# A second issuer for the expert weights: the second matrix from GpSimd's queue, the first from SyncE's

## The reference

```python
def moe_ffn(x2, w_router, b_router, w_mlp1, b_mlp1, w_mlp2, b_mlp2):
    logits = x2.astype(F32) @ w_router.astype(F32) + b_router.astype(F32)
    top_val, top_idx = lax.top_k(logits, TOP_K)        # 4 of 32
    gate = jax.nn.softmax(top_val, axis=-1)
    ...
    def expert_block(args):
        tok, gb, e = args
        hmid = x2[tok] @ w_mlp1[e] + b_mlp1[e]         # 1024 x 2048
        glu = jnp.minimum(hmid[:, :D_FF], SWIGLU_LIMIT)
        lin = jnp.clip(hmid[:, D_FF:], -SWIGLU_LIMIT, SWIGLU_LIMIT)
        act = glu * jax.nn.sigmoid(SWIGLU_ALPHA * glu) * (lin + 1.0)
        y = act @ w_mlp2[e] + b_mlp2[e]                # 1024 x 1024
        return y.astype(F32) * gb[:, None]
```

## Time and profile before

| | us |
|---|---|
| median of 3 runs | 1462.99 (1461.76 to 1463.04) |
| the profiled execution | 1465.3 |
| its span | 1463.5 |
| PE busy | 1387.0 (95%) |
| DVE busy | 444.8 (30%) |
| ACT busy | 271.6 (19%) |
| POOL busy | 24.5 (2%) |
| queue q1, share of 16 DMA engines | 79.1%, 458.29 MB |
| queue q0, share of 16 DMA engines | 1.4%, 5.40 MB |

### The profile page before, as it was taken

How to read it: one execution, slowest core, us unless ns; L and a number is a source line. 1 busy time by engine, 2 the same in 40 slices (tenths; PEclk the granted TensorE clock), 3 DMA queues, 4 the chain that set the end, 5 groups by cost and what they waited for, 6 DMA issues and landing times.

```text
span 1463.5 us, 18983 instructions
## 1 busy us (share of the span) xinstructions
PE 1387.0 (95%) x6775; PEld 775.3 (53%) x6775; DVE 444.8 (30%) x1164; ACT 271.6 (19%) x534; POOL 24.5 (2%) x54
## 2 busy tenths in 40 slices
PE   8999998998999999999999999999999999999998
PEld 6887777896477534434434344344343443434433
DVE  3035333534751222221321222213212132122222
ACT  4222732211302101111111011111110101101111
POOL 3000000000000000000000000000000000000000
PEclk9999988999999699999999999999999999999999
DMA  8753222113396299999999999999999999999996
GB/s 269 232 173 123 85 88 69 49 58 122 115 323 225 95 407 400 419 416 418 418 418 417 417 419 418 419 416 416 419 418 419 416 418 418 418 418 416 419 417 253
DMA packets 119362, 464.38 MB, mean 317 GB/s; under 512 B 7555, under 2 KB 43501, under 8 KB 86512
## 3 DMA queue, kind: packets, MB, share of 16 engines
q1 hardware_dynamic: 117632, 458.29, 79.1%
q0 software_dynamic: 1520, 5.40, 1.4%
q10 hardware_dynamic: 176, 0.22, 0.1%
HBM read 459.09 MB, written 5.83 MB: 318 GB/s over the span
## 4 chain that ended last, share of the span: by engine, by line
PE 73%; DMA 13%; SPq 6%; DVE 4%; ACT 2%; issue 2%; DVEq 0%; ACTq 0%
PE bank L612 69%; DMA ring<-in_w_mlp 12%; SPq L483 6%; PE bank L616 4%; DVE arena L2013 0%; ACT arena L1509 0%; DMA arena<-in_x_prompt 0%; DVE arena L2019 0%; DVE arena L2022 0%; ACT arena L1383 0%; ACT arena L1246 0%; ACT ring L1268 0%; ACT arena L1382 0%; DVE arena L2015 0%; DVE arena L1864 0%
## 5 line engine op out<-in xcount | busy, mean ns | idle before, releaser
L612 PE MATMUL bank<-ring,arena 128*64 128x512 f32 (+3 forms) x3296 | 714.3, 582 | 41.5 <-ACT arena L1509 22.2
L612 PEld LDWEIGHTS bank<-ring,arena 128*64 128x64 f32 (+2 forms) x3296 | 242.6, 138 | 478.5 <-issue 428.2
L612 PE MATMUL bank<-arena 128*128 128x128 f32 (+9 forms) x1748 | 347.2, 338 | 17.0 <-DVE arena L1864 3.8
L612 PEld LDWEIGHTS bank<-arena 128*128 128x128 f32 (+4 forms) x1748 | 251.3, 192 | 123.3 <-issue 47.3
L612 PE MATMUL bank<-arena,ring 128*128 128x264 f32 (+1 forms) x1136 | 269.2, 394 | 2.5 <-ACT ring L1268 1.2
L612 PEld LDWEIGHTS bank<-arena,ring 128*128 128x128 f32 x1136 | 216.4, 195 | 48.8 <-issue 11.3
L2001 DVE COPY arena<-bank 128x512 f32<-128x512 f32 x32 | 22.1, 692 | 530.6 <-PE bank L612 530.6
L616 PE MATMUL bank<-arena 128*128 128x128 f32 (+6 forms) x587 | 88.2, 286 | 11.6 <-DMA arena<-in_x_prompt 5.9
L1513 ACT ACTIVATE arena<-bank 128x512 f32<-128x512 f32 x32 | 19.1, 597 | 381.1 <-PE bank L612 381.1
L616 PEld LDWEIGHTS bank<-arena 128*128 128x128 f32 (+6 forms) x587 | 67.6, 145 | 32.5 <-issue 18.0
L1509 ACT ACTIVATE arena<-bank 64x512 f32<-64x512 f32 x63 | 37.3, 592 | 197.8 <-PE bank L612 197.1
(11 more groups left out here) (318 smaller groups left out, 431.0 us busy)
## 6 DMA issues: line engine op xcount, KB each, us to landing
ring<-in_w_mlp SPq DMA_DIRECT2D x384, 1024.0 KB, 19.6
ring<-in_w_in SPq DMA_DIRECT2D x25, 1024.0 KB, 5.2
ring<-in_w_branch SPq DMA_DIRECT2D x6, 1024.0 KB, 7.9
ring<-in_w_mem_kv SPq DMA_DIRECT2D x4, 1024.0 KB, 15.9
ring<-in_cache_mem_k SPq DMA_DIRECT2D x4, 1024.0 KB, 5.4
ring<-in_cache_mem_v SPq DMA_DIRECT2D x4, 1024.0 KB, 6.6
ring<-in_w_out SPq DMA_DIRECT2D x4, 1024.0 KB, 9.0
out_gdn_s<-arena POOLq DMA_DIRECT2D x2, 1024.0 KB, 8.8
```

The lines of the kernel that those rows point to most:

```text
L612: return nc.tensor.matmul(out, lhsT, rhs, start=start, stop=stop, skip_group_check=True)
```

## The change

The load of an expert is split by matrix. SyncE keeps the eight pieces of the first matrix with the same waits and the same loops. The four pieces of the second matrix are issued by GpSimd, behind all of its other work, in loops of their own with the same waits for `mm2`; for expert 0 they wait for nothing of their own, since GpSimd has waited for `merged` (24) at L597 already. For that, GpSimd also waits for `items_ready` and reads the number of items and their experts. Slots, semaphores and the sizes and shapes of the transfers are the same.

```diff
-        def load_expert(e, item):
-
-            for p in range(SLOTS):
+        def load_first_matrix(e, item):
+
+            for p in range(8):
                 s = expert_slot(p)
                 if item is None:
-                    sp.wait_ge(*at(*(release[N_PRE - PRE_SLOTS + p] if p < PRE_SLOTS else ("merged", 24))))
-                elif p < 8:
+                    sp.wait_ge(*at(*release[N_PRE - PRE_SLOTS + p]))
+                else:
                     sp.wait_ge(*at("mm1", item * 8 - 8 + (p + 1)))
-                else:
-                    sp.wait_ge(*at("mm2", item * 4 - 4 + (p - 7)))
...
+                sp.dma_start(ring[:, s, :], w1[bass.ds(e, 1), p, :, :].rearrange("e p n -> p (e n)")).then_inc(landed[s], 16)
...
         pool.dma_start(y_e[0:N_EXP, :], A["b_mlp2"][0]).then_inc(sem("b2_landed"), 16)
+
+        w2 = A["w_mlp2"][0].rearrange("e (j k p) n -> e j p k n", p=P, k=2)
+
+        def load_second_matrix(e, item):
+
+            for j in range(4):
+                s = expert_slot(8 + j)
+                if item is not None:
+                    pool.wait_ge(*at("mm2", item * 4 - 4 + (j + 1)))
+                src = w2[bass.ds(e, 1), j, :, :, :].rearrange("e p k n -> p (e k) n")
+                pool.dma_start(grid(ring[:, s, :], D), src).then_inc(landed[s], 16)
+
+        load_second_matrix(0, None)
+        with pool.Fori(1, N_EXP) as e:
+            load_second_matrix(e, e)
+        pool.wait_ge(*at("items_ready", 1))
+        n_loop = pool.value_load(item_count[0:1, 0:1], min_val=N_EXP // 2 - 1, max_val=(N_EXP + EXTRA) // 2 - 1)
+        with pool.If(n_loop > N_EXP // 2 - 1):
+            with pool.Fori(N_EXP, n_loop * 2 + 2) as item:
+                e = pool.value_load(item_expert[0:1, bass.ds(item, 1)], min_val=0, max_val=N_EXP - 1)
+                load_second_matrix(e, item)
```

More of the change, by code:

```diff
@@ L464, in _ @@
         w1 = A["w_mlp1"][0].rearrange("e (k p) n -> e k p n", p=P)
-        w2 = A["w_mlp2"][0].rearrange("e (j k p) n -> e j p k n", p=P, k=2)
-        def load_expert(e, item):
-            for p in range(SLOTS):
+        def load_first_matrix(e, item):
+            for p in range(8):
                 s = expert_slot(p)
                 if item is None:
-                    sp.wait_ge(*at(*(release[N_PRE - PRE_SLOTS + p] if p < PRE_SLOTS else ("merged", 24))))
-                elif p < 8:
+                    sp.wait_ge(*at(*release[N_PRE - PRE_SLOTS + p]))
+                else:
                     sp.wait_ge(*at("mm1", item * 8 - 8 + (p + 1)))
-                else:
-                    sp.wait_ge(*at("mm2", item * 4 - 4 + (p - 7)))
[L477 to L485, removed]
+                sp.dma_start(ring[:, s, :], w1[bass.ds(e, 1), p, :, :].rearrange("e p n -> p (e n)")).then_inc(landed[s], 16)
+        load_first_matrix(0, None)
         with sp.Fori(1, N_EXP) as e:
-            load_expert(e, e)
+            load_first_matrix(e, e)
         sp.wait_ge(*at("items_ready", 1))
@@ L492, in _ @@
                 e = sp.value_load(item_expert[0:1, bass.ds(item, 1)], min_val=0, max_val=N_EXP - 1)
-                load_expert(e, item)
+                load_first_matrix(e, item)
         y_p = O["y_p"][0].rearrange("(c p) d -> p c d", p=P)
```

## The result

The changed kernel takes 1476.69 us (median of 5 runs, 1473.49 to 1479.05) against 1463.04 us (5 runs, 1461.76 to 1464.11) for the one before, a ratio of 1.0092 [1.0073, 1.0111]. It is slower by 13.7 us; 7.5 us were forecast.

The account below looks back on a forecast made before the run. Late pairs were taken as bound by the DMA stream at 418 GB/s, early ones by TensorE. Delivery order +7.5 us, all else 0, on the profiled 1465.3 gave 1472.8, less 2.3 to the median: 1470.5 us, range 1455 to 1488.

Parts of the forecast that it names:

- The direction and what bounds: Expert loop: late pairs bound by the DMA stream at 418 GB/s, early ones by TensorE; slower, chance 0.66.
- term for order: Expert loop: second-matrix requests run beside first-matrix pieces needed sooner; +7.5 us, taken between 8.7 and 5.5.
- upper case of 8.7 us: Last expert: both queues get the same bytes, the first matrix lands last at 1448.6 us, wanted at 1439.9; 8.7 us.
- the second case: Last expert: queues alternate by packets, first matrix gets two thirds of the bytes and lands late; 5.5 us.
- PE waiting for first-matrix pieces only: Expert loop, sign of the forecast: TensorE waits only for first-matrix pieces, by some 18 us in all.
- far below that of the first: Late pairs, sign of the forecast: second matrix's landing time far below the first's; before, both about 20 us.
- The pattern: Expert loop: pairs of 60.2 to 60.3 us begin at about 730 us in place of 968.
- GpSimd's side: GpSimd: 128 added issues of 1.15 to 1.19 us, 4.8 us per 30 us expert; cost 0, at worst 0.5 us.
- VectorE: VectorE's short loop steps (0.294 us) beside GpSimd's issues: holding each other up costs 0 to 0.5 us.
- a faster stream by a second queue: Load stream: two queues fill each other's gaps; 2% more stream gives 1452 us; chance 0.20.
- a slower one by the software queue: Load stream: late or dearer software-queue descriptors thin it; 1% gives 1480 us, 2% 1489; chance 0.19.
- if PE waits for the second matrix: Expert loop: TensorE waiting for second-matrix pieces was named as a sign that the forecast is wrong; no size.

Follow-up runs that it names:

- e3: Changed kernel with pieces split odd and even: SyncE issues 0, 2, .., 10, GpSimd 1, 3, .., 11; 1464.72 us, ratio 1.0013.
- e7: Changed kernel loading only the first half of each second-matrix piece from expert 1 on; 1450.99 us, ratio 0.9927.
- e9: Changed kernel with the second matrix in 8 KB rows, hidden units permuted in the transposes' stationary operand; 1464.34 us, ratio 1.0003.
- e8: Kernel before, one SyncE queue, second matrix in 8 KB rows, hidden units permuted in the transposes' stationary operand; 1456.50 us, ratio 0.9955.
- e1: Changed kernel with all twelve pieces of every expert issued by GpSimd in one queue, in order of need; 1462.97 us, ratio 1.0003.
- e11: e8 plus first matrix in 16 KB rows (2 MiB DMAs), features permuted where ScalarE writes token rows before the loop; 1453.07 us, ratio 0.9924.
- e5: Kernel before, one queue, second matrix in 8 KB rows, the first layer's moving operand read in steps of 2; 1474.46 us, ratio 1.0077.
- e2: Changed kernel with queues exchanged: GpSimd issues the first matrix, SyncE the second; 1474.72 us, ratio 1.0078.
- e10: e8 plus first matrix in 16 KB rows (2 MiB DMAs), features permuted in the gather's stationary operand; 1460.22 us, ratio 0.9985.

## Why the prediction was right, and where not

- *The direction and what bounds* were right: the stream stays at 418 GB/s, one queue is in the order of need already, a second one only disturbs it. e3 and e7 show both halves: keep the order, or take the load off the stream, and the cost goes.
- *Size of the term for order.* Forecast +7.5 us; measured +13.7 us between the medians, and in the profiled execution +14.9 us in the loop (less 3.4 us of luck before it). Where the queues do get the same bytes, the forecast's upper case of 8.7 us stands beside 7.8 us measured between e9 and e8.
- *Why 7.5 and not 5.5.* The prediction leaned towards equal bytes because in the earlier trace rows the software queue filled 62.7% of the engines' time against 42.8%. The same rows give it 0.27 of 0.93 MB, less than a third: time was read where bytes were meant. The case of equal bytes did not occur in this kernel, and the case that occurred was priced at 5.5 us, so that 7.5 us came nearer to 13.7 is luck.
- *The step that failed* is the second case, "if the queues alternate by packets ... d = 5.5 us". The alternation was right, what followed from it was worked out for the last first matrix alone. With a third of the bytes, the 4 MiB of the second matrix need 3 x 10.0 = 30 us beside a full first queue. The fourth slot of a pair's second expert is free at 679.0 us and the same slot is wanted again at 703.7, 25 us later; it took 27. The four pieces together took 31.5 us, from the first issue at 674.5 us to 706.05. So the second matrix is the late one, contrary to "PE waiting for first-matrix pieces only". Nor is its landing time "far below that of the first": the medians are 16.1 against 14.3 us over the whole run, and 16.8 against 18.3 us from 1380 us on. The late second matrix also makes the stream work ahead on the first matrix, whose pieces lie unused while TensorE waits. That is why the stream is over 31 us before the end. In the last pair TensorE waits 3.95 us for the second matrix of the first of its two experts and not at all for the first matrix on which both cases of the prediction were worked out.
- *A term that was not in the sum* is TensorE's clock. In the profiled execution matmuls after five of the waits took 1.5, 1.3, 2.6, 1.3 and 1.6 us longer than at full clock, 8.3 us beside the 15.8 us of waiting. e9, whose longest wait is 1.35 us, has none of this.
- *The pattern* was wrong with it: not even pairs of 60.26 us from 730 us on, but one long wait in about three pairs. The sum of free and long pairs must still follow the stream: the ten pairs from 671.97 to 1276.88 us average 60.49 us, the pace of the stream being 60.26.
- *GpSimd's side* was right: issues took 0.70 us, less than the 1.15 us of the earlier trace rows, and e1 shows that three times as many cost nothing. *VectorE* was right too: its clamp still takes 293 to 295 ns, and e7 shows no loss.
- *The rivals*: a faster stream by a second queue and a slower one by the software queue are refuted by e1 and e3. Of what would make me wrong, "if PE waits for the second matrix" came true; the forecast of the sign stood on the part of the argument that did not need it.

How much of the 14.9 us would be gone without the 8.3 us at the lower clock is open. It was not tried alone, and since the stream runs on meanwhile, part of it is likely given back in the pairs that follow, except in the last.

## What to carry to other kernels

When a load stream is full, what counts is the order in which it delivers. One queue in the order of use was the best of the orders tried here; before splitting it, ask for each piece how long it takes at its queue's share of the bytes against the time from its slot's release to its next use, at every place of the loop and not at the last alone. While both queues had work the share went by packets, so the queue with smaller rows got less. And rows of 8 or 16 KB per partition gave this stream more (422 and 426 GB/s against 418) than any placement of the issues; the permutation that they need has to lie where it costs little, in the transposes' stationary operand (e8) or outside the loop (e11), not in the moving operand (e5).

## What was not expected of the hardware

*The clock after a wait.* In the changed kernel, TensorE's eight matmuls after a wait of 2.42 us took 3.48 us in place of 1.94, at a mean granted clock of 0.54, that is near the lower level of 1.2 GHz:

```profile
703.68:706.10 2.42, 0.00 (x1) 0.00 (x1) 0.91 (x6) 0.00 (x0) 0.70 (x1) 1.00 1.02 423
706.10:709.58 3.48, 3.48 (x8) 0.68 (x8) 1.50 (x6) 0.00 (x0) 0.00 (x0) 0.54 1.02 417
```

After 3.95 us it was 3.50 us, and after 4.22 us 3.27 us. A wait of 2.03 us, in the pair from 1033 us, cost more behind it: the next eight took 2.77 us, and after one more gap the first layer took 15.75 us in place of 13.95, its first 3.8 us at a granted clock of 0.52:

```profile
1067.19 2.77 PE L624 MATMUL bank<-ring,arena 128*64 128x512 f32 x8 [2.03 <-DMA ring<-in_w_mlp]
1071.34 15.75 PE L624 MATMUL bank<-ring,arena 128*64 128x512 f32 x64 [1.38 <-ACT arena L1521]
```

```profile
1071.34:1075.14 3.80, 3.80 (x10) 1.26 (x12) 0.00 (x0) 0.00 (x0) 0.00 (x0) 0.52 1.02 418
```

In e2, after 2.13 us, it was 2.67 us and then 15.85 us for the first layer. After 1.34 us in e9, and after 1.93 us in e2, the eight took 1.94 us as ever. So one wait of 2.03 to 2.42 us costs 4 to 5 us at once, while the waits before the change cost only themselves:

```profile
1374.51 1.94 PE L612 MATMUL bank<-ring,arena 128*64 128x512 f32 x8 [0.56 <-DMA ring<-in_w_mlp]
```

A wait is not the only occasion. In e10, where TensorE waits for no weights and was busy without a break from 1025 us, the clock fell at 1031 us, and 96 matmuls took 22.52 us in place of 20.82; what set it off there is open:

```profile
1031.00:1036.00 5.00, 5.00 (x18) 1.69 (x19) 0.43 (x1) 0.88 (x3) 0.00 (x0) 0.66 1.03 408
```

*The step of an operand.* A moving operand in steps of 2 cost 0.67 us in a first layer of 64 matmuls; the stationary operand of the transposes in steps of 2 cost 0.16 us in a whole pair (58.71 against 58.55), that of the gather 0.31 us (59.02 against 58.71).
